# Low halves of thirty weight units: a subtraction on Pool, or a negated copy on ScalarE and an adding transfer

## What is computed

```python
h2 = rms_norm(x, norm2_g[l]) * (1.0 + sc2) + sh2
q = (ht @ peer_wq).reshape(T, PEER_HEADS, 2, PEER_DH)          # the query units
s = jnp.einsum('thpd,hpkd->thpk', q, peer_keys)                # the key scores
sv, si = lax.top_k(s, PEER_TOPK)                               # the selection
...
top, pos = lax.top_k(cand, PEER_TOPK)
...
a = gelu(jnp.einsum('td,thkd->thk', hb, peer_u[ib]))           # 16384 experts
y = jnp.einsum('thk,thkd->td', gb * a, peer_v[ib])
```

## Time and profile before

| | us |
|---|---|
| median of 3 runs | 1608.56 |
| lowest and highest | 1607.56, 1610.56 |
| the profiled execution | 1606.33 |
| its span | 1604.5 |
| busy in the span: TensorE | 1582.9 (99%) |
| busy: VectorE | 1338.7 (83%) |
| busy: ScalarE | 634.6 (40%) |
| busy: Pool | 406.6 (25%) |

### The profile page before, as it was taken

One profiled execution on the slowest core, in us unless ns is written; L12 is line 12 of the kernel. 1 busy time (PEld: TensorE's weight loads), 2 busy tenths in 40 slices (PEclk: granted clock), 3 DMA queues, 4 the chain that ended last, 5 costly groups with the idle time before them and its releaser, 6 DMA issues.

```text
span 1604.5 us, 24652 instructions
## 1 busy us (share of the span) xinstructions
PE 1582.9 (99%) x8490; PEld 1382.4 (86%) x8490; DVE 1338.7 (83%) x2533; ACT 634.6 (40%) x978; POOL 406.6 (25%) x343
## 2 busy tenths in 40 slices
PE   8999999999999999999999999999999999999998
PEld 4777678887889999999998888888888888888887
DVE  6899787774899999999678888888888888888876
ACT  5433834235334445554333333333333333333332
POOL 0000001102435200001244334433343333433420
PEclk9999999999999999999999999999999999999999
DMA  9431245753324467868999999999999999999981
GB/s 339 144 106 40 99 165 185 254 185 120 109 82 151 156 208 251 279 227 259 387 413 387 352 345 332 333 360 358 343 331 328 357 356 349 329 326 359 355 312 69
DMA packets 168012, 418.79 MB, mean 261 GB/s; under 512 B 12673, under 2 KB 78337, under 8 KB 167810
## 3 DMA queue, kind: packets, MB, share of 16 engines
q1 hardware_dynamic: 115472, 247.92, 42.4%
q0 software_dynamic: 42960, 156.79, 27.3%
q10 hardware_dynamic: 9506, 13.12, 2.2%
HBM read 375.83 MB, written 41.95 MB: 260 GB/s over the span
## 4 chain that ended last, share of the span: by engine, by line
PE 94%; DVE 3%; ACT 1%; issue 1%; DMA 0%; DVEq 0%; ACTq 0%
PE bank L1575 18%; PE bank L1577 17%; PE bank L1576 17%; PE bank L1921 11%; PE bank L1922 11%; PE bank L1920 11%; PE bank L1899 3%; PE bank L1831 1%; DVE sb_scr L1086 1%; PE bank L1748 1%; PE bank L1607 1%; PE bank L1738 1%; PE bank L1609 1%; PE bank L1608 1%; DVE sb_scr L987 1%
## 5 line engine op out<-in xcount | busy, mean ns | idle before, releaser
L625 ACT ACTIVATE sb_w_hi<-sb_stage 128x1024 fp32r<-128x1024 f32 x324 | 343.2, 1061 | 541.8 <-PE bank L1922 323.7
L973 DVE TENSOR_TENSOR sb_w_lo<-sb_stage,sb_w_hi 128x1024 fp32r<-128x1024 f32 x294 | 359.4, 1224 | 169.8 <-ACT sb_w_hi L625 168.6
L1575 PE MATMUL bank<-sb_act_hi,sb_w_hi 128*128 128x384 f32 (+1 forms) x1408 | 498.1, 354 | 2.9 <-DVE sb_w_lo L973 2.2
L1577 PE MATMUL bank<-sb_act_hi,sb_w_lo 128*128 128x384 f32 (+1 forms) x1408 | 492.7, 350 | 0.0
L1576 PE MATMUL bank<-sb_act_lo,sb_w_hi 128*128 128x384 f32 (+1 forms) x1408 | 492.2, 350 | 0.0
L1922 PE MATMUL bank<-sb_w_hi,sb_mix_lo 128*128 128x512 f32 x768 | 300.1, 391 | 0.0
L1921 PE MATMUL bank<-sb_w_lo,sb_mix_hi 128*128 128x512 f32 x768 | 299.9, 391 | 0.0
L1920 PE MATMUL bank<-sb_w_hi,sb_mix_hi 128*128 128x512 f32 x768 | 298.8, 389 | 0.0
L1575 PEld LDWEIGHTS bank<-sb_act_hi,sb_w_hi 128*128 128x128 f32 x1408 | 264.4, 188 | 23.3 <-issue 4.4
L1576 PEld LDWEIGHTS bank<-sb_act_lo,sb_w_hi 128*128 128x128 f32 x1408 | 264.5, 188 | 17.3 <-issue 0.5
L1577 PEld LDWEIGHTS bank<-sb_act_hi,sb_w_lo 128*128 128x128 f32 x1408 | 264.2, 188 | 15.2
(11 more groups left out here) (244 smaller groups left out, 1814.6 us busy)
## 6 DMA issues: line engine op xcount, KB each, us to landing
sb_stage<-u_dram SPq DMA_DIRECT2D x128, 512.0 KB, 5.5
sb_stage<-v_dram SPq DMA_DIRECT2D x128, 512.0 KB, 6.0
sb_stage<-w_front_dram SPq DMA_DIRECT2D x68, 512.0 KB, 4.4
g_scratch<-sb_scr SPq DMA_DIRECT2D x12, 2048.0 KB, 8.8
sb_scr<-g_scratch SPq DMA_DIRECT2D x32, 768.0 KB, 8.0
sb_scr<-w_ada_dram POOLq DMA_DIRECT2D x32, 512.0 KB, 4.6
a_scratch<-sb_scr ACTq DMA_DIRECT2D x64, 192.0 KB, 4.0
sb_scr<-a_scratch SPq DMA_DIRECT2D x16, 768.0 KB, 11.7
```

The lines of the kernel that those rows point to most:

```text
L625: nc.scalar.activation(w_hi[:, slot, :], stage[:, slot, :], ACT.Copy).then_inc(w_round, 1)
L973: nc.vector.tensor_tensor(w_lo[:, slot, :], stage[:, slot, :], w_hi[:, slot, :].bitcast(F32), ALU.subtract).then_inc(w_split, 1)
L1575: nc.tensor.matmul(out, w_hi[:, slot, w], rhs_hi[:, dc, :], start=(i == 0), stop=False)
L1577: last = nc.tensor.matmul(out, w_lo[:, slot, w], rhs_hi[:, dc, :], start=False, stop=(i == len(dcs) - 1))
```

## The change

Pool's subtraction goes for units 54 to 83. In its place ScalarE makes, right behind the rounding of such a unit, a second copy of stage with the factor -1 into w_lo (in fp32r, so it is minus w_hi), counted by w_neg. Pool waits for that and issues a transfer that adds stage to what stands in w_lo (sum_unit); its landing is counted by one of four semaphores w_sum. When it has landed, Pool counts w_split (sum_done). Pool issues the transfer of unit n+1 before it waits for that of unit n. The store of x2 now stands between the transfers of units 55 and 56. The hardware loop over the rest becomes straight code.

```diff
+        w_neg = sem("w_neg")
+        w_sum = [sem(f"w_sum{i}") for i in range(RING)]
...
-            def split_unit(n, slot):
-                pool.wait_ge(w_round, n + 1)
-                if isinstance(n, int):
-                    pool.wait_ge(w_split, n)
-                else:
-                    pool.nop(nofuse=True)
-                nc.gpsimd.tensor_tensor(w_lo[:, slot, :], stage[:, slot, :], w_hi[:, slot, :].bitcast(F32),
-                                        ALU.subtract).then_inc(w_split, 1)
-
-            for n in range(POOL_FIRST, WQ0 + 4):
-                split_unit(n, n % RING)
+            def sum_unit(n):
+
+                pool.wait_ge(w_neg, n - POOL_FIRST + 1)
+                pool.dma_start(w_lo[:, n % RING, :], stage[:, n % RING, :].bitcast(F32R), accum_op=ALU.add
+                               ).then_inc(w_sum[n % RING], 16)
+
+            def sum_done(n):
+
+                pool.wait_ge(w_sum[n % RING], 16 * ((n - POOL_FIRST) // RING + 1))
+                pool.wait_ge(w_split, n)
+                pool.nop(nofuse=True).then_inc(w_split, 1)
+
+            sum_unit(POOL_FIRST)
+            for n in range(POOL_FIRST, WQ0 + 3):
+                sum_unit(n + 1)
+                sum_done(n)
 
             pool.wait_ge(a_pre, 2 * DC)
             pool.dma_start(x2_d.rearrange("c p t -> p c t"), x[:, :, :]).then_inc(x2_out, 16)
-            with pool.Fori(WQ0 // RING + 1, POOL_LAST // RING) as turn:
-                for slot in range(RING):
-                    split_unit(turn * RING + slot, slot)
+            for n in range(WQ0 + 3, POOL_LAST):
+                if n + 1 < POOL_LAST:
+                    sum_unit(n + 1)
+                sum_done(n)
...
             nc.scalar.activation(w_hi[:, slot, :], stage[:, slot, :], ACT.Copy).then_inc(w_round, 1)
+            if isinstance(nn, int) and POOL_FIRST <= nn < POOL_LAST:
+                nc.scalar.activation(w_lo[:, slot, :], stage[:, slot, :], ACT.Copy, scale=-1.0).then_inc(w_neg, 1)
```

## The result

| | us |
|---|---|
| kernel before, median of 20 runs (lowest, highest) | 1608.58 (1607.08, 1611.57) |
| kernel after, median of 20 runs (lowest, highest) | 1612.89 (1610.11, 1615.53) |
| ratio, 95% interval | 1.0023, 1.0017 to 1.0029 |
| profiled execution of after, its span | 1614.75, 1612.9 |

A forecast was written before the change was run, and what follows sets the result against it. TensorE, busy 99% of the span, was taken to bound the kernel. Terms 0 + 0 + 0 + 2.2 us, the last a wait at unit 56, took the median from 1608.56 to 1610.8 us; range 1607.5 to 1624.

The forecast's parts named there:

- What bounds, and no gain: Whole kernel: TensorE bounds, never waits for Pool's low halves, so removing thirty subtractions gains 0; gain as rival, chance 0.03.
- The second copy at 0: ScalarE, units 54 to 83: thirty negated copies, 28.5 us together, fit its idle time and cost 0.
- The price: Adding transfer within SBUF: 2.9 us of engine time, twice a load's 1.44, and 6.1 us to land.
- S: Time of the sixteen DMA engines per adding transfer: taken as 2.9 us, bounds 1.44 and 5.8.
- L: Latency of an adding transfer until it lands: taken as 6.1 us, bounds 4.6 and 9.
- The collision at unit 56: Query stage: unit 56's transfer queues behind x2's store on Pool, so TensorE waits 2.2 us.
- 402.7 + S: Forecast time in us at which x2's store lands, ahead of unit 56's transfer.
- The slab stage at 0: Units 71 to 83: adding transfers land in time for TensorE, costing 0 us.
- A unit's own chain: Slab stage, unit 73: from rounding through copy and transfer to TensorE's need, the landing may take 9.5 us.
- The cycle of the stage buffer: Slab stage: four slabs, 16.64 us, for load, rounding, copy, signalling and sum; the landing may take 10.3 us.
- the first rival: Slab stage: DMA engines saturate, +2.7 to +9.5 us; with x2's wait 1613.5 to 1620.3 us; chance 0.30.
- the slow path: Adding transfers need 5.8 us of engine time: 8 us at x2, +54 in slabs, about 1662 us; chance 0.19.

The follow-up runs named there:

- the kernel with both causes away: Changed kernel, but ScalarE issues x2's store and Pool subtracts again for slab units 71 to 83; 1609.22 us, ratio 0.9997 to the kernel before.

## Why the prediction came out as it did

**What bounds, and no gain: right.** With the low halves left out altogether the time is that of before. VectorE's contention did go: the 96 instructions of what was line 1291 now read

```profile
L1301 DVE TENSOR_TENSOR sb_scr<-sb_wide x96: 174/177/204, 406.7 to 538.1; 128x16 f32<-128x16 f32 x32, 128x24 f32<-128x24 f32 x32, 128x48 f32<-128x48 f32 x32
...
DVE sb_scr L1399 <- POOLq L585: 13.4, 1, 13.4
```

The maximum of 2405 ns has become 204, and VectorE gave all of it back in one wait for unit 83 (13.4 us; 9 were forecast).

**The second copy at 0: right in this kernel, for an incomplete reason.** The list of what is queued behind the copy on ScalarE was complete and each cover held. What it left out is the engine whose *start* the copy moves: with a Pool subtraction behind it, a delay of some 1 us was enough to lay that over a VectorE add and cost a 1.4 us wait.

**The price: right.** S = 2.9 us stands against 3.0 in the query stage. The first transfer, with idle engines, landed in 4.8 us; L = 6.1 against a median of 6.4 in the query stage. What the Trainium skill says (Collectives: The Full Stack, The bandwidth ceiling: the fold count and why AG ≠ RS ≠ AR), that an add costs two source reads where a copy costs one, agrees with the copy's taking half the price; that it is the read and not the arithmetic no run here separates. By the estimate from its figure S would be 2.0 us and the wait 0.4, and the measured 3.0 and 2.05 us decide against that.

**The collision at unit 56: right, 2.2 forecast and 2.05 measured.** The steps held too. On Pool's timeline,

```profile
393.79 1.22 POOL L593 DMA_DIRECT2D x_scratch<-sb_x  x1
396.62 0.86 POOL L578 DMA_DIRECT2D sb_w_lo<-sb_stage  x1 [1.61 <-ACT sb_w_lo L635]
...
x_scratch<-sb_x POOLq DMA_DIRECT2D x1, 2048.0 KB, 14.1
```

x2 lands at 393.79 + 14.1 = 407.9. The forecast's 402.7 + S, with the 1.7 us by which this execution's key scores began later, gives 407.3. Unit 56's sum lands at 396.62 + 13.7 = 410.3, and TensorE goes on at 410.44. Taking the store out of the way removed the wait on either of two ways.

**What the wait brings with it: missing.** The forecast priced a 2.2 us wait at 2.2 us. In both profiles of the changed kernel the granted clock fell right behind it (0.62 and 0.75 over four microseconds), another 1.6 us; in the one with the sums in the query stage alone it didn't, though it has the same wait of 2.1 us. In none of the ten profiles without the wait was the clock under 1.00 from 400 to 420 us. That the wait makes the fall likely is what these few profiles suggest; when it does and when not stays open.

**The slab stage at 0: wrong.** This is the step that failed: "L may be 9.5 us", and "All of this costs 0 at L = 6.1." L was the landing with engines that have room. What was in hand spoke against that: 0.59 of the engines' time was taken already, and S = 2.9 of 4.16 us is another 0.70. A unit's own chain held: 8.7 us, and 9.2 at most in that stage, against 9.5. The cycle of the stage buffer did not. It leaves 16.64 - 1.06 - 0.95 - 0.4 = 14.2 us for a load and a sum; the prediction put 3.9 + 6.1 = 10.0 there, and the measured medians are 5.9 + 8.7 = 14.6. By the engines' time it comes out alike. With the measured prices a slab needs 2.64 us for the sum (59.4% of 40 us over 9.0 transfers), 1.5 for the load (30.7%, 8.1 loads) and 0.58 for the stores (14.0% of 4.16), together 4.7, where full engines gave 1.04 x 4.16 = 4.3. The missing 0.4 us over 13 slabs are 5.2, of which the margin of 9.5 - 6.1 = 3.4 hides most: 1.8 us left. Measured: 2.7, 0.8, 1.2, 1.3 and 1.7 us in the five kernels with sums in the slabs. This is the first rival at its low end (+2.7, from a rate under 400 GB/s on; after moved 273, with the sums' second read of 118 that makes 391). The rival and the forecast's wait were not alternatives; both came, and their sum of 1613.5 at the rival's lower end stands against 1612.89. That it comes so near is in part luck, since the second profile has 0.8 us in the slabs and the fall of the clock is in neither term. The rival's upper end took 344 GB/s from a stretch of another mix and was far off, and the slow path is excluded by S = 3.0.

## What to carry to other kernels

Before work moves to a transfer, add its engine time to the share already taken in each stage, and use a landing time measured with full engines wherever the sum passes 1; the landing of an idle stage is a lower bound. Look at what stands ahead of the transfer in its queue, in bytes: a store nobody waits for becomes everybody's wait. An instruction that costs nothing on its own engine can still push another engine's work over a third's; list what starts later because of it, and not only what is queued behind it.

## What the runs showed of the hardware

- An adding transfer within SBUF of 512 KB takes Pool 0.86 us to issue (min and median 856 ns, max 906), against 0.53 for a plain load, 4.8 us to land with idle engines, 8.7 with full ones, and 3.0 us of the sixteen engines in the half-loaded query stage (2.64 with full ones) against 1.5 for the copy.
- The engine time of a load isn't fixed, and it doesn't simply fall or rise with the share: 1.5 us each at a share of 0.23 (22.6% of 60 us for nine), 1.9 at 0.58 (45.4% of 40 us for 9.8, the kernel with both causes away), 1.5 at 1.04 (30.7% of 40 us for 8.1, after). Shares added from stages that aren't full can overstate the need: 0.59 + 0.70 would have said 1.29, the full stage needed about 1.14 (4.7 of 4.16 us).
- A VectorE add of 128 x 512 took 1.99 instead of 0.68 us beside Pool's subtraction of 128 x 1024; it was 1.31 us longer, and Pool's instruction had 1.45 us left when it began.
- TensorE's wait of 2 us at unit 56 was followed, in two profiles of three, by 4 us at a granted clock of 0.62 and 0.75, so its price there was some 1.6 us more than itself. Falls of the same kind stand around the norm, between 375 and 389 us, in seven of the thirteen profiles, so a fall behind a wait isn't by itself the wait's.
